# The mixer's opening: first products from the unscaled input, the row put on their results

## The reference, cut to what matters

```
def rmsnorm(x, g):
    xf = x.astype(jnp.float32)
    y = xf * lax.rsqrt(jnp.mean(xf * xf, axis=-1, keepdims=True) + EPS)
    return (y * g.astype(jnp.float32)).astype(x.dtype)
...
z = rmsnorm(x, g_mix) @ w_in          # 1024 -> 2304 columns
za, zb, zc = parts of z
out = concat(conformer_conv(za), short_gated_conv(zb), spatial_gating(zc)) @ w_out
```

## Time and profile before

| what | value |
|---|---|
| median of 3 runs | 2965.97 us (2964.48 to 2967.8) |
| profiled execution, first to last instruction | 2966.1 us |
| TensorE matmuls busy | 2631.9 us (89%) |
| VectorE busy | 1948.1 us (66%) |
| GpSimd busy | 1676.7 us (57%) |
| ScalarE busy | 822.5 us (28%) |
| granted TensorE clock, mean | 0.969 |

### The profile page before, as it was taken

One profiled execution on the slowest core, in us unless ns is written; L12 is line 12 of the kernel. 1 busy time (PEld: TensorE's weight loads), 2 busy tenths in 40 slices (PEclk: granted clock), 3 DMA queues, 4 the chain that ended last, 5 costly groups with the idle time before them and its releaser, 6 DMA issues.

```text
span 2966.1 us, 32442 instructions
## 1 busy us (share of the span) xinstructions
PE 2631.9 (89%) x9809; PEld 1213.2 (41%) x9809; DVE 1948.1 (66%) x3967; ACT 822.5 (28%) x1792; POOL 1676.7 (57%) x1024
## 2 busy tenths in 40 slices
PE   7989888888887888878787989999999988999999
PEld 3454333333333333333333774444444434444444
DVE  7947777777777777777878673566335685566523
ACT  2423222222222222222233551222112245222101
POOL 5544444444444444544445857777776641677776
PEclk9999999999999999999998979999999998999999
DMA  4259999999999999999962323233332310233322
GB/s 139 67 202 416 421 422 421 416 408 421 415 419 412 410 410 419 415 413 402 422 248 60 95 58 102 92 99 107 111 97 86 120 59 8 72 105 99 121 96 82
DMA packets 133098, 696.15 MB, mean 235 GB/s; under 512 B 29867, under 2 KB 31180, under 8 KB 67052
## 3 DMA queue, kind: packets, MB, share of 16 engines
q0 software_dynamic: 73728, 536.90, 43.9%
q1 hardware_dynamic: 59244, 157.74, 16.4%
HBM read 686.72 MB, written 7.86 MB: 234 GB/s over the span
## 4 chain that ended last, share of the span: by engine, by line
PE 31%; DMA 25%; POOLq 16%; DVE 14%; issue 8%; ACT 3%; DVEq 2%; POOL 1%; ACTq 0%; SPq 0%
DMA R<-expert_uv_dram,idx 25%; PE bank L555 19%; POOLq L2604 8%; PE bank L769 8%; POOLq L2602 7%; DVE R L2044 3%; DVE Z L2066 1%; POOL R L2629 1%; DVE xt L2328 1%; ACT Z L1336 1%; DVE R L1789 1%; PE bank L1090 1%; DVE R L2436 1%; DVE R L2056 0%; DVE ci L1990 0%
## 5 line engine op out<-in xcount | busy, mean ns | idle before, releaser
L769 PE MATMUL bank<-R,Z 128*128 128x512 f32 x2048 | 968.8, 618 | 231.7 <-ACT Z L1336 227.3
L2629 POOL DMA_INDIRECT R<-expert_uv_dram,idx x512 | 596.0, 1164 | 722.5 <-PE bank L769 671.4
L555 PE MATMUL bank<-R 128*128 128x512 f16 (+1 forms) x4320 | 955.3, 382 | 14.6 <-DVE R L1773 7.0
L2044 DVE SCALAR_TENSOR_TENSOR R<-R 128x1024 f32<-128x1024 f32 x512 | 622.8, 1222 | 198.6 <-DMA R<-expert_uv_dram,idx 196.1
L769 PEld LDWEIGHTS bank<-R,Z 128*128 128x128 f32 x2048 | 381.1, 195 | 802.7 <-issue 415.4
L2601 POOL TENSOR_TENSOR R<-wring,beat 128x1024 f16<-128x1024 f32 (+2 forms) x223 | 456.8, 2048 | 427.1 <-PE bank L555 379.7
L555 PEld LDWEIGHTS bank<-R 128*128 128x128 f16 (+1 forms) x4320 | 420.5, 98 | 547.8 <-issue 33.8
L2603 POOL TENSOR_TENSOR R<-wring,R 128x1024 bf16<-128x1024 f32 (+2 forms) x223 | 520.3, 2333 | 32.4 <-issue 0.3
L1336 ACT ACTIVATE Z<-consts,R 128x128 f32<-128x128 f32 x512 | 177.6, 394 | 321.7 <-DVE R L2056 321.7
L555 PE MATMUL bank<-Z,R 128*128 128x512 f16 x1104 | 239.9, 379 | 1.5 <-POOLq L2604 1.5
L1329 ACT ACTIVATE R<-R 128x2 f32<-128x2 f32 x256 | 52.1, 203 | 606.1 <-DVEq L2046 605.8
(11 more groups left out here) (356 smaller groups left out, 2467.5 us busy)
## 6 DMA issues: line engine op xcount, KB each, us to landing
wring<-up_dram SPq DMA_DIRECT2D x88, 512.0 KB, 3.5
wring<-down_dram SPq DMA_DIRECT2D x32, 704.0 KB, 4.0
wring<-ple_dram SPq DMA_DIRECT2D x16, 640.0 KB, 3.8
wring<-w_in_dram SPq DMA_DIRECT2D x18, 512.0 KB, 3.5
R<-expert_uv_dram,idx POOLq DMA_INDIRECT x512
wring<-glu_dram SPq DMA_DIRECT2D x16, 512.0 KB, 3.6
Z<-w_q_dram SPq DMA_DIRECT2D x11, 512.0 KB, 8.0
wring<-ple_a_dram SPq DMA_DIRECT2D x8, 640.0 KB, 6.0
```

Of the source, the lines that this page charges most:

```text
L555: mm = pe.matmul(bank[:, :], low(w) if i else w, low(v) if j else v, start=(start and c == 0 and p == 0), stop=(stop and c == n - 1 and p ...
L769: mm = pe.matmul(banks[2 * par + c][:, :], diag[:, k % 4, :], pairs[:, slot, 1, c * SEQ:(c + 1) * SEQ], start=(k == 0), stop=(k == TOPK - 1))
L2044: dot = ve.scalar_tensor_tensor(pairs[:, slot, 0, :], pairs[:, slot, 0, :], 1.0, ntok[:, T, :], ALU.mult, ALU.mult, accum_out=act[:, par, ...
L2629: po.indirect_dma_start(pairs[:, slot, :, :].rearrange("p a b -> p (a b)"), None, A["expert_uv"], bass.IndirectOffsetOnAxis(idx[:, n % 2, ...
```

## The change

The first three slabs are multiplied with gain times unscaled input, whose parts (`XU`) lie in an arena that is free in this stage until later. Their results are multiplied by the row in their banks. The scaled tiles `xs` are made as before, but later, and are first used by the fourth slab. The columns `g_mix` are sent ahead of the input tiles, and the first slab of `w_in` ahead of the constants. ScalarE and VectorE make the parts of the first three unscaled tiles between the third and the fourth square and those of the other five while the row is made; ScalarE copies the row to `S_row` after the sixth. TensorE issues the first three tiles' matmuls ahead of the spread of the row and the other five behind it. VectorE multiplies the first two results between scaled tiles and the third behind them; ScalarE takes the first result between its high parts.

```
-            for k in range(KT):
+            sp.dma_start(col("g_mix", 0, KT), A["cols"][...]).then_inc(loaded, 16)
+            for k in range(KT):
                 sp.dma_start(hT[:, k, :], A["xT"][:, k, :]).then_inc(tile_landed[k], 16)
+            sp.dma_start(wring[...], A["w_in"][0]).then_inc(w_full[s0 % NSLOT], 16)
+            sp.wait_ge(loaded, 16)
             sp.dma_start(consts[:, :], A["consts"]).then_inc(loaded, 16)
-            sp.dma_start(cols[:, :], A["cols"]).then_inc(loaded, 16)
+            sp.dma_start(cols[:, KT:], A["cols"][:, KT:]).then_inc(loaded, 16)
...
# TensorE
-            pe.wait_ge(loaded, 32)
-                norm_stats(NORM["mixer"])
+                pe.wait_ge(ss_ready, NORM["mixer"] + 1)
+                row_means(sumsq, stat_bank)
...
+                    if i == 0:
+                        product(bank, slot, 0, FIRST_TILES, XU, gn_ready, G0["mixer"], stop=False)
+                        norm_spread(NORM["mixer"], inv, scale_bank)
+                        product(bank, slot, 0, KT - FIRST_TILES, XU, gn_ready, ..., order=range(FIRST_TILES, KT))
+                    if i < UNSCALED:
+                        product(..., XU).then_inc(mm_done, 1)
...
# ScalarE
+                    if k == FIRST_TILES - 1:
+                        ac.wait_ge(loaded, 16)
+                        for j in range(FIRST_TILES):
+                            gain_high("mixer", j)
...
                 norm_root(NORM["mixer"])
-                high_parts("mixer", xs)
+                for j in range(FIRST_TILES, KT):
+                    gain_high("mixer", j)
+                    if j == 5:
+                        ac.wait_ge(rb_mm, NORM["mixer"] + 1)
+                        ac.activation(S_row, scale_bank[:, :], ACT.Copy).then_inc(s_ready, 1)
+                high_parts("mixer", xs, lambda k: input_out(0) if k == 5 else None)
...
# VectorE
-                norm_apply("mixer", "g_mix")
+                norm_scale(NORM["mixer"])
+                for j in range(FIRST_TILES, KT):
+                    gain_low("mixer", j)
+                ve.wait_ge(s_ready, S_READY["mixer"])
+                norm_tiles("mixer", lambda k: col("g_mix", k), xs, a_ready,
+                           lambda k: scaled(0) if k == 3 else scaled(1) if k == KT - 2 else None)
+                scaled(2)
+                ve.wait_ge(loaded, 48)
```

More of the change, by code:

```diff
@@ L53 @@
 WSLOT = 11 * P
-OPENS = {"ple_a": "ple_a", "up0": "up0", "ple0": "ple0", "attn": "w_k", "up1": "up1", "ple1": "ple1"}
+OPENS = {"mixer": "w_in", "ple_a": "ple_a", "up0": "up0", "ple0": "ple0", "attn": "w_k", "up1": "up1", "ple1": "ple1"}
 NSLOT = NBANK = 4
@@ L183, in build @@
         XO = parts_of(row(aT), 0, KT, SEQ)
[L184 removed]
+        XU = parts_of(R, 5232, KT, SEQ)
+        UNSCALED = FIRST_TILES = 3
+        GAINS = {"mixer": (("g_mix", XU),), "ple_a": (("g_ple", XO),), "up0": (("ffn_norm0", XA),), "ple0": (("ple_norm0", XC),), "attn": (("kv_norm", xs), ("attn_norm", XA)),
                  "up1": (("ffn_norm1", XA),), "ple1": (("ple_norm1", XC),)}
         G0 = {name: KT * sum(len(GAINS[m]) for m in list(GAINS)[:i]) for i, name in enumerate(GAINS)}
[L187 to L188 removed]
+        S_READY = {"mixer": 1, "ple_a": 2, "up0": 3, "ple0": 4, "attn": 6, "up1": 7, "ple1": 8}
+        SC0 = {"mixer": 0, "ple_a": UNSCALED, "up0": UNSCALED + KT, "ple0": UNSCALED + KT + 2 * FT,
+               "up1": UNSCALED + 2 * KT + 2 * FT, "ple1": UNSCALED + 2 * KT + 4 * FT}
         S_row = sq[:, 1, :]
         gn_hi, gn_ready, s_ready, sc_done, col_mm = [sem(n) for n in ("gn_hi", "gn_ready", "s_ready", "sc_done", "col_mm")]
[L191 removed]
+        SCALED = [name for name in NORM if name == "mixer" or name != "final_a" and name not in GAINS]
         SQUARES = [name for name in ("mixer", "peer", "final_a", "up0", "ple0", "attn", "up1", "ple1") if name in NORM]
@@ L402, in _, with stream @@
         def _(sp):
-            def stream(name, ahead=False, rest=False):
+            def stream(name, ahead=False, rest=False, begun=0):
                 s0, n = SLAB0[name], SLABS[name]
@@ L408, in stream @@
                 straight = n if s0 % NSLOT or n % NSLOT else NSLOT if s0 - NSLOT < FIRST or ahead or rest else 0
-                for i in range(0 if rest else straight):
+                for i in range(begun, 0 if rest else straight):
                     s = s0 + i
@@ L705, in _ @@
                         continue
-                    product(banks[(t0 + i) % NBANK], (s0 + i) % NSPLIT, 0, KT, xs, a_ready if i == 0 else None,
+                    if i == 0:
+                        bank, slot = banks[t0 % NBANK], s0 % NSPLIT
+                        product(bank, slot, 0, FIRST_TILES, XU, gn_ready, G0["mixer"], stop=False)
+                        norm_spread(NORM["mixer"], inv, scale_bank)
+                        product(bank, slot, 0, KT - FIRST_TILES, XU, gn_ready, G0["mixer"] + FIRST_TILES, start=False,
+                                first_of_slab=False, order=range(FIRST_TILES, KT)).then_inc(mm_done, 1)
+                        continue
+                    if i < UNSCALED:
+                        product(banks[(t0 + i) % NBANK], (s0 + i) % NSPLIT, 0, KT, XU).then_inc(mm_done, 1)
+                        continue
+                    product(banks[(t0 + i) % NBANK], (s0 + i) % NSPLIT, 0, KT, xs, a_ready if i == UNSCALED else None,
                             KT * SCALED.index("mixer")).then_inc(mm_done, 1)
@@ L1182, in norm_root, with high_parts @@
                 ac.activation(root2 if i == NORM["ple_a"] else root, stat_bank[0:NT, 0:P], ACT.Sqrt, bias=eps[0:NT, :]).then_inc(rs_ready, 1)
-            def high_parts(name, parts):
+            def high_parts(name, parts, beside=None):
                 base = KT * TILED.index(name)
@@ L1189, in high_parts @@
                     ac.activation(parts[:, k, 0, :], tile_banks[k % 2][:, :], ACT.Copy).then_inc(hi_done, 1)
+                    if beside:
+                        beside(k)
             def scale_out(name, row):
@@ L1263, in _ @@
                 for i in range(TILES["w_in"]):
[L1264 to L1267, removed]
+                    if i:
+                        input_out(i)
                     if i == 8:
@@ L1764, in norm_scale, with norm_tiles @@
                 ve.drain().then_inc(ri_ready, 1)
-            def norm_tiles(name, gain, parts, ready):
+            def norm_tiles(name, gain, parts, ready, beside=None):
                 base = KT * TILED.index(name)
@@ L1839, in _, with scaled @@
                     gather_square("mixer", k)
-            ve.wait_ge(loaded, 32)
+                    if k == FIRST_TILES - 1:
+                        for j in range(FIRST_TILES):
+                            gain_low("mixer", j)
             barrier(ve, "setup")
             if stage("mixer"):
-                norm_apply("mixer", "g_mix")
+                norm_scale(NORM["mixer"])
+                for j in range(FIRST_TILES, KT):
+                    gain_low("mixer", j)
+                ve.wait_ge(s_ready, S_READY["mixer"])
+                def scaled(i):
+                    scale_tile("w_in", TILE0["w_in"] + i, S_row).then_inc(sc_done, 1)
+                norm_tiles("mixer", lambda k: col("g_mix", k), xs, a_ready,
+                           lambda k: scaled(0) if k == 3 else scaled(1) if k == KT - 2 else None)
+                scaled(2)
+                ve.wait_ge(loaded, 48)
                 ve.tensor_tensor(center[:, :], ident, blk64, ALU.subtract)
```

20 lines of the change are left out of this document (14 added, 6 removed).

## The result

The changed kernel takes 2972.05 us (median of 12 runs, 2969.12 to 2973.47) against 2966.26 (12 runs, 2961.81 to 2969.27): ratio 1.0018, 95% interval 1.0010 to 1.0026. That is 5.3 us more by the ratio, inside the 5.9 us that I had called indistinguishable and outside the range of 2961 to 2969. With the same two programs run again on another occasion the ratio was 1.0019 (1.0010 to 1.0028). The loss is small, but neither interval reaches 1. Every interval given is the 95% one, and every ratio is against runs of the kernel before from the same occasion.

A forecast was written before the change was run, and what follows sets the result against it. VectorE, with 2.45 us of slack against TensorE, was taken to bound the mixer's stage. Gains of 0.95 (steps 7 and 8) and 1.45 (step 9), less 0.4 for the clock, gave 2.0 us won: 2964.0 us, range 2961 to 2969.

The forecast's parts named there:

- Steps 1 to 3: Mixer's opening: gains sent first end the sums 0.6 us later; high and low parts fit ScalarE's stall at no cost.
- Step 4: Mixer's opening: the first slab lands at about 11.9 instead of 14.76 us, and its split is ready at 16.1.
- Step 5: TensorE's opening: nine matmuls take 3.8 us from 16.1, then the row's spread 1.2 to 2.1, ending about 21.5.
- Step 7: VectorE ahead of the convolutions: small operations on constants add 1.3 us; convolutions start 1.45 us later, not earlier.
- Steps 8 and 9: Mixer's middle and tail: VectorE 0.95 us ahead, TensorE's lead shrinks to 3.2; tail wins 1.45, second reciprocal 134.4 against 136.8.
- TensorE's lead did not pass through: Rival for the mixer's stage: TensorE's whole 6.0 us lead passes through because VectorE keeps up, giving 2960.1 us; chance 0.06.
- the rival's place: Rival: clock falls in TensorE's new waits, before the transposes and the last spread, 8.5 us lost, 2972.2 us; chance 0.06.

The follow-up runs named there:

- before + 11: The kernel before with 11 hidden instructions of 0.06 us added on VectorE behind w_out: 2973.20 us, ratio 1.0021.
- The padding: Small hidden VectorE instructions behind w_out: kernel before with 11, 1.0021, with 15, 1.0008; changed kernel with 4, 1.0000, with 9, 1.0006. Kernel before, 11 behind attention: 1.0003.
- the cut kernels: Both kernels cut behind the product of w_out, fourteen stages left out: kernel before 193.77 us, changed kernel 194.70 us.
- the padded kernels before: The kernel before with hidden VectorE instructions: 11 behind w_out 2973.20 us, 15 behind w_out 2968.98 us, 11 behind attention's product 2967.55 us.
- The changed kernel later by 1.46 us: The changed kernel with 1.46 us more work on VectorE ahead of its second reciprocal: 2972.27 us, ratio 1.0018.

## Why the prediction was wrong

**The step that failed** is the sentence behind the sum, "After the stage nothing changes but the start": a term put at nothing. In the first pair of profiles the stage brought 1.5 us up to the first gather, the expert layer took 2.0 more and attention 3.7 more, which makes the 4.2 us of the two spans. In attention it is 76.1 to 76.2 us in every profile in which the pause stands ahead of that one operation, in kernels of both kinds, and 69.1 to 72.5 in all others. (By attention its last part is meant, as in the table.) The chain begins link by link: the number of instructions ahead moves the pause (before + 11), the pause loses the port by 0.3 us (0.35 becomes 1.96 us), TensorE waits 1.17 us. VectorE is then 1.6 us later than in the kernel before.

It does not stay so. 20 us behind the start of this part the 1.6 are down to 0.6; they are 1.5 at 34.5 us, the second pause among them, and 3.9 at 39.5, after two waits of VectorE for TensorE: the 1.33 us shown above, where there was none, and 2.49 us instead of 1.53. In the changed kernel TensorE has the lower clock over these 10 us (granted 0.50 from 2479 to 2489), in the kernel before the higher. The whole part in one row, columns as in the earlier trace rows: changed kernel, kernel before, kernel before in its second profile.

```profile
2453.80:2529.93 76.13, 63.40 (x274) 35.85 (x273) 40.71 (x121) 38.61 (x101) 10.88 (x12) 0.80 0.02 8
```

```profile
2453.26:2525.72 72.46, 59.86 (x274) 33.95 (x273) 38.96 (x120) 38.55 (x101) 11.06 (x12) 0.84 0.03 8
```

```profile
2452.63:2521.78 69.15, 57.38 (x273) 33.11 (x273) 38.76 (x121) 38.42 (x101) 11.06 (x12) 0.88 0.02 8
```

The same matmuls keep TensorE busy for 63.40, 59.86 and 57.38 us: 3.5 of the 3.7 us, and 2.5 of the 3.3 between the two profiles of one program. In all fourteen profiles the length of attention follows the time at the lower clock, 30.7, 23.9 or 17.1 us. The padding shows that the place of the pauses decides between the longest form and the others: four of four with the lock, none of ten without. That the wait of 1.17 us is what brings on the lower clock is argued from their order, not shown. The second pause stands as idle time of VectorE in the same four profiles, but it comes some 9 us after that stretch has begun. What decides between 72.5 and 69.1 us, with the same program and the pause in the same place, stays open.

The Trainium skill, "Runtime: NRT & Kernel Launch", section "Instruction fetch mechanics", says that an engine's instructions come in blocks, refilled while it executes, and that crossing a block's edge is mostly hidden. Pauses at fixed places in the stream fit such edges; here they are 0.40 to 0.49 us long and not hidden. That they are edges was not measured.

**Steps 1 to 3** were right: row of means 0.8 later (0.6 forecast), high and low parts hidden in the stall. **Step 4**: the slab landed at 13.1, not 11.9, and pushed the nine matmuls from 16.1 to 17.36. **Step 5** was right in size (4.02 and 1.18), but I took 1.2 to 2.1 for the spread as an uncertainty of its price. It is a fork: where it takes 2.07, late tiles of slab 0 are also at the lower clock, and slab 1 comes 2 to 3 us later (three of the five profiles of the whole changed kernel whose opening is not edited have this form). A term with two values was summed as a mean. **Step 7**: the small operations took 3.2 us, not 1.3, because I had not asked of them, as I had of the gates, where their inputs lie. **Steps 8 and 9** were right in kind: no gain by the gates' start, TensorE's lead cut at the transposes (to 2.3, forecast 3.2), four operations of the tail locked. Of the gain, the tail gave 1.25 us (1.45 forecast), but VectorE came to it 0.05 us ahead instead of 0.95, since it had begun later than step 7 says. Two slips change nothing: fifteen stages follow the mixer's, not sixteen, and step 9's terms add up to 134.2, not 134.4.

**The rivals.** TensorE's lead did not pass through. The clock did fall at the transposes, the rival's place, in four of the eight profiles of changed kernels (in the second one, granted 0.50 from 106.3 to 109.6), and nothing was lost by it up to the second reciprocal, which came at 135.14. What did cost was the clock of the opening, 2 to 3 us in some of the executions. The loss beyond that came from no rival.

**The change by itself.** With the pause ahead of the same reciprocal the kernel before has 1.0008 (0.9999 to 1.0017) and the changed one 1.0000 (0.9991 to 1.0008): no difference that these runs can tell, and none by the cut kernels either (194.7 against 193.8, with the spread told above). No version was faster than the kernel before.

**Left open**: the expert layer, from its first gather to its last, took 1295.8 to 1296.6 us in three kernels before and 1296.9 to 1298.4 in the changed ones, but also 1297.4 to 1297.9 in the padded kernels before. One of these has its padding behind attention, so its instructions up to there are those of the kernel before, and it took 1.4 us more than the first profile: much of the 2 us of the first pair lies within what the same instructions show. Earlier starts were not kept; which of its instructions decides was not looked for. The changed kernel later by 1.46 us, at 1.0018 with the pause moved, fits the account only by the long form of its opening in one profile.

## What to carry to other kernels

Where an effect under 0.3% is to be read, compare the start of the same instruction at the boundaries of stages in two or more profiles of each kernel, and pad the engine's stream with a few hidden instructions: if the ratio follows the padding, it says nothing about the change. Ask of every VectorE operation that moves, small ones too, whether both inputs lie in SBUF while GpSimd reads it; an operation on 8 columns took 2.08 us instead of 0.15. When a term hangs on a clock that has two levels, carry two sums and not their mean.

## What the runs showed of the hardware

VectorE pauses 0.40 to 0.49 us ahead of record 5103 (counted from 0), whichever instruction that is, in thirteen of thirteen profiles of whole kernels in which nothing else was waited for at that place. Against the same instruction at another number that is 0.36 us more, and the same 0.35 to 0.37 us show at 4719 (thirteen of fourteen profiles), 4847 (nine), 4975 (nine), 5231 (five) and 5359 (thirteen). `both_gains`, 128 x 8 with both inputs in SBUF, took 0.15 us in the seven profiles where no split of GpSimd ran beside it and 1.84 to 2.08 in the eleven where one did. The same matmuls of attention's last part kept TensorE busy for 57.4 to 63.4 us, by how long the lower clock was granted. Five fp32 matmuls ahead of the row of means brought it to 1.04 us from 1.87, but after 2.16 us of idle time the next nine matmuls took 3.65 of the 4.02 us again.
